# Second products of the gated feed-forward stages as seven block products, and their finish in another place: one Trainium2 core

## The chip, the cores and the metric

The kernel is one program on one core of a Trainium2 chip. Its time is the device time of one execution in microseconds (us). TensorE does the matrix products, VectorE (DVE), ScalarE (ACT) and GpSimd (POOL) the elementwise work, and SyncE (SP) issues the transfers from the chip's memory. Each engine runs its own instructions in the order in which they were written, and waits for others by semaphores.

## The reference

`reference` computes twelve half-layers on 512 tokens of width 1024, all in float32. Four of them are the gated feed-forward layers that the change touches:

```python
def swiglu_ffn(x, g, w_in, w_out):
    h = rms_norm(x, g)
    gate, up = jnp.split(h @ w_in, 2, axis=-1)
    return (jax.nn.silu(gate) * up) @ w_out
...
x = x + 0.5 * swiglu_ffn(x, ffn1_norm[layer], ffn1_w_in[layer], ffn1_w_out[layer])
```

`w_in` is 1024 x 5632 and `w_out` 2816 x 1024. The other stages are two mixers, and a second block of two layers whose modulation vector is `silu(c) @ w_mod + b_mod`, a 1024-vector by a 1024 x 6144 matrix for each layer.

## The kernel before

**Numbers.** Every float32 product is made of three products of rounded halves: each operand is split into a high part (ACT copies it to the type fp32r) and a low part (DVE subtracts the high part), and TensorE computes high x high, high x low and low x high. Names end in `h` and `l` for the two parts.

**Units.** Weights come in *units* of 128 x 1024 (or 128 x 768) in one stream for the whole program, numbered u. SP loads unit u into `raw[u % 4]` (RING = 4) when the unit four before it has been split; ACT makes `wh[u % 4]` as soon as TensorE is through with unit u - 4 (step `load`, `weights(u)`), DVE makes `wl[u % 4]`. The steps are planned so that unit u + 3 (AHEAD = 3) is split while TensorE is at unit u. A unit of 128 x 1024 is 8 tiles, so 24 matmuls of 512 columns.

**A gated stage** (`F1_0`, `F2_0`, `F1_1`, `F2_1`) has 22 tiles of 128 of the inner width in three parts of 8, 8 and 6 (`PARTS`). For each tile there are a `gate` and an `up` unit (a *pair*). Step `evac` finishes a tile: DVE multiplies both products by `rstd` from PSUM, ACT applies silu, POOL multiplies, ACT makes `a0h` or `a1h` and DVE `a0l` or `a1l` (two buffers, by part). Step `down` multiplies one unit of `w_out` with the tiles of a part and `add` adds half of it to `x`. `plan_ffn` writes the order: gate and up of parts 0 and 1, down of part 0, gate and up of part 2, down of part 1, down of part 2. So 16 units stand between the last tile of a part and the use of it, or 8 for part 2.

**Modulation.** DVE computes the modulation vectors on the side in the gated stages: 54 steps `mod` each, of which 48 are a *fold* (one weight tile of 256 KB, loaded by SP into one of three slots when the fold three before it is done) and 6 a transpose and a sum. A pair has one, a down unit two.

**Groups.** The ungated stages (`REL_0`, `REL_1`) already have their second products in *groups*: two output tiles, two times 4 tiles of the inner width, and two halves of the tokens (`SOONER`, `LATER`) make a product of 2 x 2 blocks by 2 x 2 blocks, done with seven block products instead of eight, as Strassen's method does. It needs sums of weight blocks (`first_sum` to `fourth_sum`, then their high and low parts in `low_sums`, `low_fourth`, `low_dif`) and sums of blocks of `a` (`t`, kept in `a1h` and `a1l`), and afterwards sums of the results. There the weight sums of a group are made in two sets of slots while TensorE is in the group before it.

## Time and profile before

| | |
|---|---|
| runs | 3074.09 us median of 3 (3073.77 to 3079.27) |
| the profiled execution | 3072.16 us, of which 3070.4 us are the span from the first to the last instruction |
| granted clock of TensorE | 0.997 of full speed |
| TensorE busy | 3035.4 us, 99% |
| VectorE busy | 1884.7 us, 61% |
| ScalarE busy | 1168.8 us, 38% |
| DMA | 33.2% of 16 engines, 107 GB/s |

Matmuls overlap in the profile: one lasts 390 ns, but the next starts before it ends, so what one costs is the distance from start to start. The same holds in a smaller measure on VectorE and ScalarE, where instructions in a row start some 0.09 us before the one ahead has ended. Rows of the line of time have the start first and then how long.

### The profile page before, as it was taken

The page shows a single profiled execution, that of the slowest core. Times are in us where ns is not written, and L with a number is a line of the kernel's source. Part 1 is how long each engine was busy: PE and PEld are TensorE (multiplying, and loading weights), DVE is VectorE, ACT ScalarE, POOL GpSimd, SP SyncE. Part 2 cuts the span into 40 slices and gives each one's busy share as a digit, 9 for nine tenths or more (in the row PEclk, how much of TensorE's full clock was granted, in tenths as well). Part 3 has the DMA queues.
Part 4 walks back from the last instruction along what each step waited for, and adds up shares of the span by engine and source line. Part 5 has one row for each costly group of instructions (what it writes and reads, how often), then busy time and mean ns, then how long its engine had stood idle before and what let it go on. Part 6 is the DMA issues. An engine that isn't in the chain of part 4 may idle for free.

```text
span 3070.4 us, 39047 instructions
## 1 busy us (share of the span) xinstructions
PE 3035.4 (99%) x15394; PEld 2499.0 (81%) x15394; DVE 1884.7 (61%) x2899; ACT 1168.8 (38%) x1877; POOL 670.0 (22%) x525
## 2 busy tenths in 40 slices
PE   9999999999999999999999999999999999999999
PEld 7888887788888888887778888776799977779997
DVE  6454557554555445536774455677777856877775
ACT  4322334333223322234443222446544334654442
POOL 2101134111011110044311100346211123721111
PEclk9999999999999999999999999999999999999999
DMA  5343432243443434431133344310333232033232
GB/s 191 117 154 123 127 98 73 86 140 118 155 130 115 137 117 154 134 108 62 35 127 117 120 155 134 115 37 21 107 103 110 98 110 67 20 95 110 97 102 77
DMA packets 115814, 329.86 MB, mean 107 GB/s; under 512 B 13616, under 2 KB 19120, under 8 KB 115248
## 3 DMA queue, kind: packets, MB, share of 16 engines
q1 hardware_dynamic: 115632, 327.36, 33.2%
q8 instruction: 123, 2.02, 0.3%
q14 instruction: 59, 0.48, 0.1%
HBM read 325.21 MB, written 2.10 MB: 107 GB/s over the span
## 4 chain that ended last, share of the span: by engine, by line
PE 92%; DVE 4%; ACT 2%; POOL 1%; issue 1%; DMA 0%; SPq 0%; DVEq 0%; ACTq 0%; POOLq 0%
PE ps L83 91%; PE ps L86 1%; ACT s_tmp L89 1%; POOL s_tmp L100 1%; DVE s_wl L92 1%; DVE s_tmp L92 1%; DVE s_tmp L112 0%; DVE s_x L95 0%; ACT s_wh L89 0%; DVE s_small L106 0%; DVE s_tmp L100 0%; POOL s_tmp L92 0%; DVE s_tmpr L92 0%; ACT s_hh L89 0%; DMA s_raw<-in_f1i_dram 0%
## 5 line engine op out<-in xcount | busy, mean ns | idle before, releaser
L83 PE MATMUL ps<-s_hh,s_wh 128*128 128x512 f32 x2304 | 894.6, 393 | 20.2 <-ACT s_hh L89 11.6
L89 ACT ACTIVATE s_wh<-s_raw 128x1024 fp32r<-128x1024 f32 (+3 forms) x560 | 530.6, 951 | 951.9 <-PE ps L83 949.7
L83 PE MATMUL ps<-s_hh,s_wl 128*128 128x512 f32 x2304 | 888.2, 391 | 0.2
L83 PE MATMUL ps<-s_hl,s_wh 128*128 128x512 f32 x2304 | 887.3, 390 | 0.0
L92 DVE TENSOR_TENSOR s_wl<-s_raw,s_wh 128x1024 fp32r<-128x1024 f32 (+3 forms) x529 | 595.9, 1127 | 428.1 <-ACT s_wh L89 427.5
L92 POOL TENSOR_TENSOR s_tmp<-s_tmp 128x512 f32<-128x512 f32 (+2 forms) x228 | 306.8, 1350 | 1692.6 <-ACT s_tmp L89 1531.7
L83 PEld LDWEIGHTS ps<-s_hh,s_wh 128*128 128x128 f32 x2304 | 433.3, 188 | 117.6 <-issue 16.8
L83 PEld LDWEIGHTS ps<-s_hh,s_wl 128*128 128x128 f32 x2304 | 433.9, 188 | 93.2 <-DVE s_wl L92 2.5
L83 PEld LDWEIGHTS ps<-s_hl,s_wh 128*128 128x128 f32 x2304 | 434.1, 188 | 90.9 <-issue 2.2
L83 PE MATMUL ps<-s_a0h,s_wh 128*128 128x512 f32 (+1 forms) x1024 | 381.8, 373 | 0.0
L83 PE MATMUL ps<-s_a0h,s_wl 128*128 128x512 f32 (+1 forms) x1024 | 378.4, 370 | 0.0
L83 PE MATMUL ps<-s_a0l,s_wh 128*128 128x512 f32 (+1 forms) x1024 | 378.4, 370 | 0.0
L83 PEld LDWEIGHTS ps<-s_a0h,s_wh 128*128 128x128 f32 x1024 | 193.0, 188 | 33.9 <-issue 1.3
L83 PEld LDWEIGHTS ps<-s_a0h,s_wl 128*128 128x128 f32 x1024 | 193.0, 188 | 32.8
L83 PEld LDWEIGHTS ps<-s_a0l,s_wh 128*128 128x128 f32 x1024 | 193.1, 189 | 32.6 <-DVE s_a0l L92 0.7
L92 DVE TENSOR_TENSOR s_a0l<-s_tmp,s_a0h 128x512 fp32r<-128x512 f32 (+1 forms) x120 | 79.8, 665 | 162.5 <-ACT s_a0h L89 162.5
L95 DVE SCALAR_TENSOR_TENSOR s_x<-ps,s_x 128x512 f32<-128x512 f32 x129 | 88.2, 684 | 118.9 <-PE ps L83 118.9
L83 PE MATMUL ps<-s_a1h,s_wh 128*128 128x512 f32 (+1 forms) x448 | 153.9, 344 | 0.0
L83 PE MATMUL ps<-s_a1l,s_wh 128*128 128x512 f32 (+1 forms) x448 | 153.9, 344 | 0.0
L83 PE MATMUL ps<-s_a1h,s_wl 128*128 128x512 f32 (+1 forms) x448 | 153.9, 344 | 0.0
L89 ACT ACTIVATE s_tmp<-ps 128x512 f32<-128x512 f32 (+6 forms) x258 | 132.3, 548 | 51.8 <-DVE s_tmp L92 20.1
L89 ACT ACTIVATE s_a0h<-s_tmp 128x512 fp32r<-128x512 f32 (+1 forms) x120 | 70.8, 590 | 190.2 <-POOL s_tmp L92 177.2
(167 smaller groups left out, 3618.7 us busy)
## 6 DMA issues: line engine op xcount, KB each, us to landing
s_raw<-in_ff_dram SPq DMA_DIRECT2D x128, 512.0 KB, 3.7
s_tmp<-in_w_mod_dram SPq DMA_DIRECT2D x192, 256.0 KB, 3.6
s_raw<-in_f1i_dram SPq DMA_DIRECT2D x88, 512.0 KB, 3.6
s_raw<-in_f2i_dram SPq DMA_DIRECT2D x88, 512.0 KB, 3.6
s_raw<-in_f1o_dram SPq DMA_DIRECT2D x32, 512.0 KB, 3.5
s_raw<-in_f2o_dram SPq DMA_DIRECT2D x32, 512.0 KB, 3.6
s_raw<-in_hyb_dram SPq DMA_DIRECT2D x28, 512.0 KB, 3.5
s_raw<-in_nsa_dram SPq DMA_DIRECT2D x28, 512.0 KB, 3.6
```

The lines of the kernel that those rows point to most:

```text
L83: return self.eng.matmul(o, w, m, **kw) if self.eng is not None else Blank()
L86: return self.eng.transpose(*a) if self.eng is not None else Blank()
L89: return self.eng.activation(o, a, f, **kw) if self.eng is not None else Blank()
L92: return self.eng.tensor_tensor(o, a, b, f) if self.eng is not None else Blank()
L95: return self.eng.scalar_tensor_tensor(o, a, s, b, f, g) if self.eng is not None else Blank()
L100: return self.eng.tensor_scalar(o, a, s, t, f) if g is None else self.eng.tensor_scalar(o, a, s, t, f, g)
```

## The change

In the gated stages the second product of parts 0 and 1 is made in groups (`lone_group`), four for each part; part 2 stays as it was. A group is two units of `w_out` and has seven blocks of 12 matmuls of 256 columns, 84 in all, where two down units had 48 of 512. `a0h` and `a0l` now hold every part, and `a1h` and `a1l` the block sums, so a part's products must be over before the next part's tiles are stored: the order becomes gate and up of part 0 and of the first tile of part 1, groups of part 0, the rest of part 1 and the first tile of part 2, groups of part 1, the rest of part 2, down of part 2.

There is one set of slots for weight sums (slots 45, 46, 48, 49, `ssum` and `ssum2`), and a group's own sums are made in the group. `raw` of a group's two units is given back to SP by the semaphore step of `low_fourth` (`raw_free`). The blocks that need `low_sums` and `low_fourth` stand last in TensorE's order. The finish of a tile is split: `evac` keeps the two DVE multiplications, silu and the product on POOL, and `fine`, after the next unit, makes the high and low parts and, for each second tile of parts 0 and 1, the block sums. The folds have two slots instead of three; no fold stands in a group, three in a pair of part 0, two in one of part 1, and four in each of four pairs of part 2. `lone_sum` adds up the kept blocks: for two output pairs right after the groups of part 1, for the two others in pairs of part 2.

```diff
+    def gate_up(p, these):
+        for i in these:
+            n = (sum(PARTS[:p]) + tile_of(p, i)) * 2
+            order.append((("gate", p, i), [stream.add(win[n], 1024)]))
+            order.append((("up", p, i), [stream.add(win[n + 1], 1024)]))
+    def down(p):
+        k0 = sum(PARTS[:p])
+        for d in range(0, KT, 2):
+            us = [stream.add(wout[d + m, :, k0 * 128:(k0 + PARTS[p]) * 128], PARTS[p] * 128) for m in range(2)]
+            if p == 2:
+                order.extend((("down", p, d + m), [us[m]]) for m in range(2))
             else:
-                steps.extend([("gate", p, t, ug), ("load", ug + AHEAD)])
-            if p == 0 and t == int(late_norm):
+                stream.group(us, True)
+                order.append((("group", p, d), us))
+    gate_up(0, range(8))
+    for p in (0, 1):
+        gate_up(p + 1, range(1))
+        down(p)
+        gate_up(p + 1, range(1, PARTS[p + 1]))
+    down(2)
...
+    for what, us in order:
+        kind, p, i = what
+        n = us[0] + AHEAD
+        steps.append((kind, p, i, us[0]))
+        if kind == "group":
+            if p == 1 and i == KT - 2:
+                steps.extend([("sum", 4), ("sum", 6)])
+            continue
+        if added:
+            steps.append(("add",) + added)
+        if n not in stream.second:
+            steps.append(("load", n))
+        if kind == "gate":
...
+            steps.append(("evac",) + before)
+        elif kind == "up":
+            fold(1 if i == 0 else (3, 2, 4)[p])
+            steps.append(("fine",) + before)
+            before = (p, i)
+            if p == 2 and i in (1, 2):
+                steps.append(("sum", 2 * i - 2))
+        elif before:
+            steps.extend([("evac",) + before, ("fine",) + before])
+            before = None
+        if n in stream.second:
+            steps.append(("load", n))
+        if added:
+            steps.append(("tile", added[1]))
+        if kind == "down":
...
+            added = (p, i)
+    steps += [("add",) + added, ("tile", added[1])]
...
         def raw_free(u):
-            if u in stream.first:
-                return g_lo[u + 1, 2]
-            return g_lo[u, 2] if u in stream.second else lo_of(u)
+            v = u + 1 if u in stream.first else u
+            return lo_of(u) if v not in stream.second else g_lo[v, 1 if v in stream.lone else 2]
         parity = {u: n % 2 for n, u in enumerate(sorted(stream.second))}
...
+            def lone_group(s, p, d, u0):
+                u1 = u0 + 1
+                c0, c1 = u0 % RING, u1 % RING
+                b0, b1, b2, b3 = group_at[u0]
+                claim(b0)
+                block(b0, LATER, wh[:, c0, 0:T], wl[:, c0, 0:T], w_hi[u0], w_lo[u0], a_part(s, p, 0, LATER))
+                block(b0, SOONER, wh[:, c1, 0:T], wl[:, c1, 0:T], g_hi[u1, 2], g_lo[u1, 2], t_part(s, p, 2)).then_inc(
+                    *g_mm.up((u0, 0)))
+                free[b0] = [(x_add, (s, p, d, "71"))]
+                claim(b1)
+                block(b1, LATER, wh[:, c0, T:2 * T], wl[:, c0, T:2 * T], w_hi[u0], w_lo[u0], a_part(s, p, 4, LATER)).then_inc(
+                    *unit.up(u0))
+                claim(b2)
+                block(b2, LATER, wh[:, c1, T:2 * T], wl[:, c1, T:2 * T], w_hi[u1], w_lo[u1], t_part(s, p, 3)).then_inc(
+                    *unit.up(u1))
+                free[b2] = [(x_add, (s, p, d + 1))]
+                claim(b3)
+                block(b3, SOONER, sums_hi(u1)[:, 0, :], sums_lo(u1)[1][:, 0, :], g_hi[u1, 0], g_lo[u1, 0], t_part(s, p, 0))
+                block(b3, LATER, sums_hi(u1)[:, 1, :], sums_lo(u1)[1][:, 1, :], g_hi[u1, 0], g_lo[u1, 0], t_part(s, p, 1)).then_inc(
+                    *g_mm.up((u0, 1)))
+                free[b3] = [(x_add, (s, p, d, "56"))]
+                block(b1, SOONER, fourth_hi(u1), fourth_lo(u1)[1], g_hi[u1, 1], g_lo[u1, 1], a_part(s, p, 4, SOONER)).then_inc(
+                    *g_mm.up((u0, 2)))
+                free[b1] = [(x_add, (s, p, d))]
             def group(s, p, d, u0):
...
+                    elif kind == "group":
+                        u0 = step[3]
+                        sums(u0 + 1)
+                        weights(u0 + 3)
+                        weights(u0 + 4)
+                    elif kind == "fine":
+                        _, p, i = step
+                        t, o = tile_of(p, i), S(33 + 2 * ((i + sum(PARTS[:p])) % 3))
+                        cols = LATER if p < 2 and t < 4 else slice(0, T)
+                        act.wait_ge(*prod[s, p, i])
+                        if p and i == 0:
+                            act.wait_ge(*unit[group_end[s, p - 1]])
+                            act.wait_ge(*g_mm[group_end[s, p - 1] - 1, 2])
+                        if p == 2 and i == 0:
+                            act.wait_ge(*x_add[s, "sum", 7])
+                        act.activation(a0h[:, t, cols], o[:, cols], ACT.Copy).then_inc(*a_hi.up((s, p, t)))
+                        if i % 2 and p < 2:
+                            for m in range(2):
+                                act.wait_ge(*t_dif[s, p, i // 2, (2, 3)[m]])
+                                act.activation(a1h[:, i // 2 * 2 + m, :], tmp[:, 24 + i // 2 * 2 + m, :], ACT.Copy).then_inc(
+                                    *t_hi.up((s, p, i // 2, m)))
                     elif kind == "tile":
                         tile(s + 1, step[1])
...
+            def lone_group(s, p, d, u0):
+                u1, n = u0 + 1, u0 + 3
+                b0, b1, b2, b3 = group_at[u0]
+                r0, r1 = PAIRS_FFN[d]
+                def keep(to, b, key):
+                    if p == 0:
+                        i = dve.tensor_scalar(to, two(B(b)), 1.0, None, ALU.mult)
+                    else:
+                        i = dve.tensor_tensor(to, two(B(b)), to, ALU.add)
+                    i.then_inc(*x_add.up(key))
+                first_sum(u1)
+                second_sum(u1)
+                fourth_sum(u1)
+                low_sums(u1)
+                dve.wait_ge(*g_mm[u0, 0])
+                keep(r0, b0, (s, p, d, "71"))
+                low_fourth(u1)
+                weights(n)
+                dve.wait_ge(*unit[u1])
+                dve.scalar_tensor_tensor(x[:, d + 1, LATER], ps[:, b2, LATER], 0.5, x[:, d + 1, LATER], ALU.mult,
+                                         ALU.add).then_inc(*x_add.up((s, p, d + 1)))
+                weights(u0 + 4)
+                dve.wait_ge(*g_mm[u0, 1])
+                keep(r1, b3, (s, p, d, "56"))
+                dve.wait_ge(*g_mm[u0, 2])
+                dve.scalar_tensor_tensor(x[:, d, :], B(b1), 0.5, x[:, d, :], ALU.mult, ALU.add).then_inc(*x_add.up((s, p, d)))
+            def lone_sum(s, d):
+                r0, r1 = PAIRS_FFN[d]
+                dve.wait_ge(*x_add[s, 1, d])
+                dve.tensor_tensor(r1[:, 1, :], r1[:, 1, :], r0[:, 1, :], ALU.add).then_inc(*x_add.up((s, d, "16")))
+                dve.scalar_tensor_tensor(x[:, d, LATER], r0[:, 1, :], 0.5, x[:, d, LATER], ALU.mult, ALU.add).then_inc(
+                    *x_add.up((s, d, "1")))
+                dve.wait_ge(*x_add[s, d, "16"])
+                dve.tensor_tensor(r1[:, 0, :], r1[:, 0, :], r1[:, 1, :], ALU.add).then_inc(*x_add.up((s, d, "165")))
+                dve.wait_ge(*x_add[s, d, "165"])
+                dve.scalar_tensor_tensor(x[:, d, SOONER], r1[:, 0, :], 0.5, x[:, d, SOONER], ALU.mult, ALU.add).then_inc(
+                    *x_add.up((s, "sum", d)))
+                dve.wait_ge(*x_add[s, "sum", d])
...
@@ -2075,12 +2243,26 @@
                             u = unit_at[s, ("gate", "up")[m], p, t]
                             dve.wait_ge(*unit[u])
                             dve.tensor_tensor(S(o), B(bank_of[u]), rstd[:, :], ALU.mult).then_inc(*gate_up_.up((s, p, t, m)))
...
+                    elif kind == "fine":
+                        _, p, i = step
+                        n, t = i + sum(PARTS[:p]), tile_of(p, i)
+                        o = S(33 + 2 * (n % 3))
+                        cols = LATER if p < 2 and t < 4 else slice(0, T)
+                        if i % 2 and p < 2:
+                            dve.wait_ge(*prod[s, p, i])
+                            block_sums(s, p, i // 2, S(33 + 2 * ((n - 1) % 3)), o)
                         dve.wait_ge(*a_hi[s, p, t])
-                        dve.tensor_tensor(ahl[p % 2][1][:, t, :], S(j), f32(ahl[p % 2][0][:, t, :]),
-                                          ALU.subtract).then_inc(*a_lo.up((s, p, t)))
+                        dve.tensor_tensor(a0l[:, t, cols], o[:, cols], f32(a0h[:, t, cols]), ALU.subtract).then_inc(*a_lo.up((s, p, t)))
+                        if i % 2 and p < 2:
+                            low_block_sums(s, p, i // 2)
                     elif kind == "add":
                         _, p, d = step
...
             def mod_load(f, n):
                 l, c, k = f // 2, 6 * (f % 2) + n // KT, n % KT
-                if n >= 3:
-                    sp.wait_ge(*mod_acc[(f,) + divmod(n - 3, KT)])
-                sp.dma_start(S(43 + n % 3), ins["w_mod"][l, k * 128:(k + 1) * 128, c * T:(c + 1) * T]).then_inc(
-                    *mod_in[n % 3].up((f, n), 16))
+                if n >= 2:
+                    sp.wait_ge(*mod_acc[(f,) + divmod(n - 2, KT)])
+                sp.dma_start(S(43 + n % 2), ins["w_mod"][l, k * 128:(k + 1) * 128, c * T:(c + 1) * T]).then_inc(
+                    *mod_in[n % 2].up((f, n), 16))
             def table(name, dst, src, key):
                 sp.dma_start(dst, src).then_inc(*tab_in[name].up(key, 16))
...
+                at_, split = steps[s][0][1], set()
                 for step in steps[s]:
                     kind = step[0]
-                    if kind == "load":
-                        weights(step[1] + RING)
-                    elif kind == "mod" and step[2] < KT and 8 * step[1] + step[2] + 3 < 48:
-                        mod_load(f, 8 * step[1] + step[2] + 3)
+                    if kind == "load" and step[1] not in stream.first | stream.second:
+                        split.add(step[1])
+                    elif kind == "group":
+                        split |= {step[3], step[3] + 1} | ({step[3] + 3, step[3] + 4} - stream.first - stream.second)
+                    elif kind == "mod" and step[2] < KT and 8 * step[1] + step[2] + 2 < 48:
+                        mod_load(f, 8 * step[1] + step[2] + 2)
+                    while at_ in split:
+                        weights(at_ + RING)
+                        at_ += 1
             def hyb(s):
```

VectorE at the last down units of part 0, before: for each unit an addition to `x`, the low part of a unit of weights and two folds.

```order
L95 SCALAR_TENSOR_TENSOR s_x<-ps,s_x 128x512 [waits pe_unit]
L92 TENSOR_TENSOR s_wl<-s_raw,s_wh 128x1024 [waits act_w_hi]
L95 SCALAR_TENSOR_TENSOR s_tmp<-s_tmp,s_c_act 128x512 [waits dve_mod_acc,in_mod2]
L95 SCALAR_TENSOR_TENSOR s_tmp<-s_tmp,s_c_act 128x512 [waits dve_mod_acc,in_mod0]
L95 SCALAR_TENSOR_TENSOR s_x<-ps,s_x 128x512 [waits pe_unit]
```

VectorE in the second group of part 0 after the change, from `first_sum` to the addition to `x` (`act_w_hi` is raised by ScalarE's copy of a unit, which waits for that unit's transfer):

```order
L96 TENSOR_TENSOR s_tmp<-s_raw 128x512
L96 TENSOR_TENSOR s_tmp<-s_tmp,s_raw 128x512 [waits dve_g_sum]
L96 TENSOR_TENSOR s_ssum<-s_raw,s_tmp 128x512 [waits dve_difference]
L96 TENSOR_TENSOR s_tmpr<-s_tmp,s_tmpr 128x1024 [waits act_sum_hi,dve_difference]
L104 TENSOR_SCALAR s_tmp<-ps 128x512 [waits pe_group]
L96 TENSOR_TENSOR s_ssum_r<-s_ssum,s_ssum_r 128x512 [waits act_sum_hi]
L96 TENSOR_TENSOR s_wl<-s_raw,s_wh 128x512 [waits act_w_hi]
L96 TENSOR_TENSOR s_wlf<-s_raw 128x512 [waits in_raw3,in_raw2]
L96 TENSOR_TENSOR s_wl<-s_wlf,s_wh 128x512 [waits act_sum_hi]
L99 SCALAR_TENSOR_TENSOR s_x<-ps,s_x 128x256 [waits pe_unit]
L96 TENSOR_TENSOR s_wl<-s_raw,s_wh 128x1024 [waits act_w_hi]
```

The folds are gone from here, and the `s_wl` of 128x1024, the first unit of the group after next, now stands behind a wait for ScalarE at the end of a row of eleven instructions; the keeping of the second pair of blocks and an addition to `x` follow it.

SyncE's queue at the end of part 0 after the change, where the transfers of the groups begin:

```order
L128 DMA s_tmp<-in_w_mod_dram 128x512 [waits dve_mod_acc] x4
L128 DMA s_raw<-in_f1o_dram 128x1024 [waits dve_sum_lo]
L128 DMA s_raw<-in_f1o_dram 128x1024
L128 DMA s_raw<-in_f1o_dram 128x1024 [waits dve_sum_lo]
L128 DMA s_raw<-in_f1o_dram 128x1024
L128 DMA s_raw<-in_f1i_dram 128x1024 [waits dve_sum_lo]
```

The units of `w_out` went out one by one before, each behind a `dve_w_lo`; now they go out in twos behind `dve_sum_lo`, the semaphore of `low_fourth`.

VectorE at the end of the gate and up pairs of a stage after the change, up to the first down unit of part 2; the last tile's finish was ahead of the eight down units of part 1 before:

```order
L99 SCALAR_TENSOR_TENSOR s_tmp<-s_tmp,s_c_act 128x512 x3
L90 STREAM_TRANSPOSE s_tmp<-s_tmp 128x512
L110 TENSOR_REDUCE s_nsm<-s_tmp 128x16
L96 TENSOR_TENSOR s_a0l<-s_tmp,s_a0h 128x512
L96 TENSOR_TENSOR s_wl<-s_raw,s_wh 128x768
L96 TENSOR_TENSOR s_tmp<-ps,s_rstd 128x512 x2
L96 TENSOR_TENSOR s_wl<-s_raw,s_wh 128x768
L96 TENSOR_TENSOR s_a0l<-s_tmp,s_a0h 128x512
L96 TENSOR_TENSOR s_wl<-s_raw,s_wh 128x768
L96 TENSOR_TENSOR s_tmp<-ps,s_rstd 128x512 x2
L96 TENSOR_TENSOR s_a0l<-s_tmp,s_a0h 128x512
L99 SCALAR_TENSOR_TENSOR s_x<-ps,s_x 128x512
```

The multiplications and the low part of the last two tiles now stand directly ahead of the first addition of part 2, with a unit of weights between them.

## Rows read from the trace of the kernel before

**Rows 1.** The page: busy time and its share of the span.

```profile
PE 3035.4 (99%) x15394; PEld 2499.0 (81%) x15394; DVE 1884.7 (61%) x2899; ACT 1168.8 (38%) x1877; POOL 670.0 (22%) x525
```

**Rows 2.** The chain of waits in order of time: start, how long, what.

```profile
9.97 411.07 PE ps L83 x1815
```

**Rows 3.** Line of time of TensorE in `REL_0`: starts of a group and of the next.

```profile
2227.14 0.28 PE L83 MATMUL ps<-s_a0h,s_wh 128*128 128x256 f32 x1
...
2237.22 0.28 PE L83 MATMUL ps<-s_a0h,s_wh 128*128 128x256 f32 x1
```

**Rows 4.** Line of time of VectorE in `REL_0`, ahead of and in the first groups.

```profile
2219.02 1.56 DVE L92 TENSOR_TENSOR s_tmp<-s_tmp 128x256 f32<-128x256 f32 x4 [0.93 <-POOL s_tmp L92]
...
2222.30 0.69 DVE L92 TENSOR_TENSOR s_tmp<-s_raw 128x512 f32<-128x512 f32 x1
2223.09 0.69 DVE L92 TENSOR_TENSOR s_tmp<-s_tmp,s_raw 128x512 f32<-128x512 f32 x1
2223.82 0.69 DVE L92 TENSOR_TENSOR s_tmp<-s_raw,s_tmp 128x512 f32<-128x512 f32 x1
2224.99 1.83 DVE L92 TENSOR_TENSOR s_tmpr<-s_tmp,s_tmpr 128x1024 fp32r<-128x1024 f32 x2 [0.47 <-ACT s_tmpr L89]
...
2227.34 0.68 DVE L92 TENSOR_TENSOR s_wlf<-s_raw 128x512 f32<-128x512 f32 x1
2228.72 0.69 DVE L92 TENSOR_TENSOR s_wl<-s_wlf,s_wh 128x512 fp32r<-128x512 f32 x1 [0.70 <-ACT s_wh L89]
...
2237.48 0.75 DVE L95 SCALAR_TENSOR_TENSOR s_x<-ps,s_mod,s_x 128x512 f32<-128x512 f32 x1
2238.14 1.22 DVE L92 TENSOR_TENSOR s_wl<-s_raw,s_wh 128x1024 fp32r<-128x1024 f32 x1
2239.28 0.48 DVE L95 SCALAR_TENSOR_TENSOR s_x<-ps,s_mod,s_x 128x256 f32<-128x256 f32 x1
```

**Rows 5.** Issues of transfers, KB each, us to landing: of 2229.44 us, and the page's.

```profile
s_raw<-in_ff_dram SPq DMA_DIRECT2D x1, 512.0 KB, 3.7
...
s_tmp<-in_w_mod_dram SPq DMA_DIRECT2D x192, 256.0 KB, 3.6
```

**Rows 6.** Line of time of VectorE in `F1_0`, a pair of part 1.

```profile
273.13 1.23 DVE L92 TENSOR_TENSOR s_wl<-s_raw,s_wh 128x1024 fp32r<-128x1024 f32 x1 [2.80 <-ACT s_wh L89]
274.27 1.28 DVE L92 TENSOR_TENSOR s_tmp<-ps,s_rstd 128x512 f32<-128x512 f32 x2
277.68 0.69 DVE L92 TENSOR_TENSOR s_a0l<-s_tmp,s_a0h 128x512 fp32r<-128x512 f32 x1 [2.13 <-ACT s_a0h L89]
```

**Rows 7.** The same pair on ScalarE: silu, high part, next weights.

```profile
274.99 0.63 ACT L89 ACTIVATE s_tmp<-s_tmp 128x512 f32<-128x512 f32 x1 [1.89 <-DVE s_tmp L92]
277.02 0.63 ACT L89 ACTIVATE s_a0h<-s_tmp 128x512 fp32r<-128x512 f32 x1 [1.40 <-POOL s_tmp L92]
277.56 1.04 ACT L89 ACTIVATE s_wh<-s_raw 128x1024 fp32r<-128x1024 f32 x1
```

**Rows 8.** VectorE in `F1_0` at down units: folds, a transpose and its sum.

```profile
300.40 1.60 DVE L95 SCALAR_TENSOR_TENSOR s_tmp<-s_tmp,s_c_act 128x512 f32<-128x512 f32 x2
...
312.35 0.70 DVE L86 STREAM_TRANSPOSE s_tmp<-s_tmp 128x512 f32<-128x512 f32 x1
...
313.69 0.48 DVE L100 TENSOR_SCALAR s_tmp<-s_tmp,s_c_act 128x512 f32<-128x512 f32 x1
```

**Rows 9.** VectorE in `REL_0`: one sum-up of kept blocks, and what follows it.

```profile
2435.91 0.88 DVE L92 TENSOR_TENSOR s_mix_tmp<-s_mix_tmp 128x256 f32<-128x256 f32 x2
...
2439.07 1.22 DVE L92 TENSOR_TENSOR s_wl<-s_raw,s_wh 128x1024 fp32r<-128x1024 f32 x1
```

**Rows 10.** Three stretches: length, busy by engine (x instructions), TensorE's granted clock, DMA.

```profile
1947.90:1951.70 3.80, 0.15 (x1) 0.01 (x1) 2.08 (x6) 3.70 (x10) 0.00 (x0) 0.83 0.57 148
1951.70:1957.00 5.30, 5.28 (x13) 4.13 (x14) 4.72 (x6) 1.53 (x2) 3.74 (x5) 0.50 0.94 355
2163.60:2172.00 8.40, 5.50 (x21) 3.80 (x22) 7.27 (x12) 4.78 (x8) 0.00 (x0) 1.00 0.62 189
```

More of the change, by code:

```diff
@@ L176, in down @@
-    def down(p, before):
-        k0 = sum(PARTS[:p])
-        for d in range(KT):
-            u = stream.add(wout[d, :, k0 * 128:(k0 + PARTS[p]) * 128], PARTS[p] * 128)
-            steps.append(("down", p, d, u))
-            if d:
-                steps.append(("add", p, d - 1))
-            steps.append(("load", u + AHEAD))
-            if before:
-                steps.append(("evac",) + before)
-                before = None
-            if p == 2 and d:
-                steps.append(("tile", d - 1))
-            if p < 2:
-                fold(2)
-            elif d == 2:
-                steps.append(("modsum",))
-        steps.append(("add", p, KT - 1))
-        if p == 2:
-            steps.append(("tile", KT - 1))
@@ new lines, in plan_ffn @@
+    gate_up(0, range(8))
[4 more added lines that the diff above has]
+    down(2)
+    ug, uu = (order.pop(0)[1][0] for _ in range(2))
+    steps += [("load", ug + AHEAD), ("first", ug, uu), ("load", uu + AHEAD)]
+    if not late_norm:
+        steps.append(("norm",))
+    fold(1)
+    before, added = (0, 0), None
+    for what, us in order:
[11 more added lines that the diff above has]
+        if kind == "gate":
+            if late_norm and (p, i) == (0, 1):
+                steps.append(("norm",))
+            steps.append(("evac",) + before)
[13 more added lines that the diff above has]
+        if kind == "down":
+            if i == 2:
+                steps.append(("modsum",))
+            added = (p, i)
```

176 lines of the change are left out of this document (95 added, 81 removed).

## The prediction

> **What bounds the kernel now.** The page first: TensorE is busy 99% of the span, VectorE 61%, ScalarE 38% [rows 1]. The chain of waits says the same: it is long runs of matmuls with no other engine between them, 1815 in 411.07 us, so 0.2265 us for one of 512 columns [rows 2]. So a cut in TensorE's work counts in full, but there is no slack: any wait of TensorE is a loss. I then read the line of time of `REL_0`, the stage that has groups already, for what a group asks of each engine, and that of `F1_0` for the pairs, and last what the clock does after idle time.
>
> **What TensorE saves.** A group of 84 matmuls of 256 columns starts 10.08 us after the one ahead of it [rows 3], 0.120 us each. Two down units are 48 x 0.2265 = 10.88. So a group saves 0.80, a stage with eight groups 6.4, the four stages 25.6. Nothing else changes on TensorE.
>
> A rule of the Trainium skill ("TensorE: Matmul & The Clock Gate", Back-to-back issue gap) gives columns/2.4 GHz plus 2.5 ns, so 215.8 and 109.2 ns; a group would then save 1.19 us. The rows have 226.5 and 120, and the sum keeps them.
>
> **VectorE in a group.** In `REL_0` the sums are made one group ahead; here they are made in the group. From starts in [rows 4], with t = 0 at `first_sum`: second 0.79, fourth 1.52, `low_sums` 2.69 (ends 3.91: two halves of 1.83 less the overlap), `keep` of block pair 71 at 3.82, `low_fourth` 4.42, done at 5.11. That semaphore gives both raw buffers back, and SP issues. The unit lands 3.65 later [rows 5], t = 8.79. ScalarE splits it in 1.06 [rows 7], and VectorE's low part of unit u0+4 starts at 9.9 and takes 1.14 to the next start [rows 4, 6]. Behind it in VectorE's order stand the keeping of pair 56 (0.6) and an addition (0.6): the next `first_sum` comes at t = 12.26. Without the transfer wait the same row of work would end near 10.36. TensorE needs 10.08. So each group comes 12.26 - 10.08 = **2.18** later than the one ahead, and TensorE waits for it in block 56, which needs `low_sums`: 6.0 us after the group's start (4 blocks of 12 and a fetch), with 4.1 us of matmuls after it. A transfer is thus freed and wanted within one group.
>
> The skill ("DMA: Bandwidth & Descriptors", Anatomy of one DMA, SWDGE path) has about 2.0 us of fixed cost plus bytes over 436 GB/s: 3.2 us for 512 KB instead of the row's 3.7. The cycle would be 11.8, and the groups still late.
>
> **Part 0.** A pair has three folds with two slots. The third fold's load starts when the first is done and takes 3.6 [rows 5]; with 0.75 for a fold [rows 8] it starts 4.38 after the first, and the three take 5.0. Add the low parts of two units, the two multiplications (starts 1.14 and 1.28 on, [rows 6]) and the tile's finish; the odd tile's, with its block sums (six operations of 128 x 256 or their like, [rows 4]), I put at 3.28. VectorE comes to the first group with `first_sum` at P + 2.95, P being the end of the pairs on TensorE. There it wants `low_sums` by P + 6.0: 2.95 + 3.91 = 6.9, so 0.9 late, then three times 2.18: **7.4**.
>
> **Part 1.** Two folds, both loaded in time: `first_sum` at P + 0.75, from three multiplications that stand behind the last matmul. The first group is on time, the others together 0.84 + 2 x 2.18 = **5.2**.
>
> **The end of a stage.** This is where most goes. When TensorE ends the last group of part 1, VectorE has 4.24 us left in it (t = 12.26 against P at t = 8.02). Then stand two `lone_sum` of 3.2 each [rows 9] and five pairs, TensorE's part of which is 48 x 0.2265 = 10.9 us each. In four of them VectorE has four side steps with two slots: four folds take 5.9, since the third and the fourth wait for loads of 3.6; three with a transpose and its sum (1.34, [rows 8]) 4.8 to 6.6, by where it stands. That is 23.2 for the four; two low parts of weights, two multiplications and a finish are 2.3 + 2.5 + 0.7 in each, 22; two more `lone_sum` 6.4. So 4.2 + 6.4 + 23.2 + 22 + 6.4 = 62.2, and 3.5 of waits for ScalarE and POOL as in [rows 6, 7]: tile (2,4) has its high part at P + 65.7. The last tile (2,5), in a pair without folds, has it at P + 70.8, and its low part at P + 71.5. Down unit 0 of part 2 needs both and would end at P + 54.4 + 4.1 = P + 58.5 unstalled. Before, eight down units, 87 us, lay between the last tile and its use; now there is one unit of weights. So TensorE stands **13.5** us: 71.5 - 58.5, and half a microsecond of matmuls that follow the last operand. Some 1.5 of it falls earlier, at the weights of the last pairs. Even with VectorE on time, the last tile costs: multiplication, silu 0.63, POOL, high part 0.63 [rows 7]: 3.4 from the first multiplication to the high part's end, 4.1 to the low part's; 277.68 - 274.27 in [rows 6] is that chain. It is exposed for 2.3.
>
> **The clock.** The stall falls in pieces of about 6.7 and 4.2 us. After 3.8 us of near idleness TensorE ran 5.3 us at a granted 0.50, 1.2 GHz; after 2.8 idle us it kept 1.00 [rows 10]. One such stretch for each stage costs half of some 5 us: **2.5**. The stalls inside groups are near 2 us each and leave it.
>
> **Sum.** For a stage 7.4 + 5.2 + 13.5 + 2.5 - 6.4 = 22.2; for four 88.8. The profiled execution took 3072.16, 2 us under the median, so 3161; I say **3160**. What a measurement here can tell from no change is about 0.2%, 6 us.
>
> Costed at nothing: POOL's work (22% busy, [rows 1]), and ScalarE's extra copies of block sums, which stand beside VectorE's folds. If ScalarE's order in a group (high sums, then `weights(u0+3)`) held VectorE back by 0.3, 20 groups would add 6. The issues of SP now wait for `low_fourth` in twos, and a w_mod load stands behind them in its queue; I count it as landed by the pair's first fold, and if it isn't, the end of a stage is another 2 later.
>
> **Rivals.**
> - *Loads of folds land in time.* Their 3.6 us [rows 5] may be spent behind the transposes, finishes and `lone_sum`s, if VectorE is so late that SP is far ahead. Then a pair of part 2 has 3.0 of folds instead of 5.9, and the end costs 5.2 instead of 13.5, the groups as above: 7.4 + 5.2 + 5.2 + 2.5 - 6.4 = 13.9, times four 56: **3128**. Against it: two slots and four folds in a row leave nothing else to do between the first and the third. Chance 0.17.
> - *The groups are not held by transfers* (cycle 10.36, 0.28 late each), only the end is late: 0.9 + 3 x 0.28 = 1.7 in part 0, 0 in part 1, at the end 13.5 - 1.9 = 11.6, since VectorE leaves the groups that much sooner, and 2.5 for the clock. Less 6.4 that is 9.4 a stage, 38 in all: **3110**. For it: in [rows 4] the unit that is split behind a group's additions starts with no wait. Against: there it was loaded a group earlier. Chance 0.1.
> - *Faster: VectorE's lateness does not reach TensorE* but at the last tile: 1.7 + 2.3 - 6.4 = -2.4 a stage, near **3062**, and 3072.2 - 25.6 = 3046.5 with no stall at all. It decides when VectorE's cycle in a group is under about 10.3 and the four folds of a pair under 4.5. For it: VectorE has 39% idle [rows 1], and a stage 360 us to spread it. Against: its order is fixed, and the waits computed above are for transfers, not for room. Chance 0.1.
> - *The short matmuls bring nothing*, when operands change with each one: at 0.1295 instead of 0.120 the 6.4 is gone. The pitch is from 84 in a row with the same change of operands [rows 3], so little speaks for it. **3186**. Chance 0.05.
> - No change within 0.2%: only where the waits chance to be 6.4 a stage, 0.02.
>
> **How the numbers follow.** The likeliest case has 0.56, with a range of its own of 3140 to 3180, from 1.9 to 2.4 for a group's lateness (20 of them, 5 either way) and 11 to 16 for an end (10 either way). The range of 8 in 10 takes in the 3128 and the 3110, with room below for an end that is shorter than its sum, and ends at the top short of the case without gain: 3096 to 3182. Faster, the fourth case, 0.1; same 0.02; slower 0.88, all the others.
>
> **What would show it.** In the profile after: matmuls of 256 columns about 0.120 apart, 2688 more of them and 1536 fewer of 512; TensorE waiting in every group but the first of part 1 for VectorE's write of `tmpr`, 2.2 us; VectorE idle about 1.5 in a group on ScalarE's `wh`, and about 3 us in each pair of part 2 on transfers of w_mod; TensorE idle over 10 us before or in the first down unit of part 2 for `a0h` or `a0l`, and PEclk dips there in four places. VectorE's busy share should grow by few points only. If VectorE shows no idle on `wh` in groups, the group cycle is wrong; if the folds of part 2 follow one another with no gap, the end is.

## The result and the profile after

| | before | changed |
|---|---|---|
| runs | 3075.51 us median of 4 (3073.77 to 3079.27) | 3159.33 us median of 4 (3156.39 to 3167.49) |
| changed / before | | 1.0275, 95% interval 1.0253 to 1.0297 |
| the profiled execution's span | 3070.4 us | 3165.4 us |
| granted clock | 0.997 | 0.985 |

The changed kernel is 2.75% slower, 84 us; 3160 was forecast. The first line of its page answers to [rows 1]:

```profile
PE 3053.2 (96%) x16546; PEld 2551.1 (81%) x16546; DVE 2192.8 (69%) x3491; ACT 1246.6 (39%) x2037; POOL 671.5 (21%) x525
```

TensorE has fewer columns to work through and is busy longer, and the granted clock is lower, so part of its work ran at the low clock; and 112 us of the span are without its work, where 35 were. Whom it waits for (the view of waits of TensorE: total, times, longest):

```profile
PE ps L87 <- ACT s_a0h L93: 25.2, 8, 3.4
PE ps L87 <- DVE s_tmpr L96: 16.5, 23, 0.8
PE ps L87 <- ACT s_tmpr L93: 12.9, 17, 1.5
PE ps L87 <- ACT s_hh L93: 11.4, 4, 3.5
PE ps L87 <- DVE s_a0l L96: 11.4, 5, 3.2
```

`s_a0h` and `s_a0l` are the last tiles of part 2, three waits in each gated stage; `s_tmpr` are a group's own weight sums. Further down stand 5.2 us on `s_a1h` and 2.8 on `s_a1l`, the block sums of a part's last tiles, all in the first groups of part 0. (`s_hh` is the start of the ungated stages.) Now one gated stage, `F2_0`, by windows. A window goes from the first matmul of a part's second product to the first behind it. Columns: length, busy (x instructions) of TensorE, its weight loads, VectorE, ScalarE, GpSimd, then the granted clock, DMA share, GB/s. Before the change, the eight units of part 0, and the units of parts 1 and 2 together:

```profile
794.47:837.99 43.52, 43.52 (x193) 36.04 (x192) 28.16 (x36) 9.64 (x10) 1.29 (x1) 1.00 0.54 175
903.27:979.87 76.60, 76.60 (x346) 63.15 (x344) 46.55 (x61) 24.46 (x32) 11.97 (x8) 1.00 0.44 133
```

After it: groups of part 0, groups of part 1, the pairs of part 2, down units of part 2:

```profile
743.96:792.33 48.37, 43.73 (x337) 42.16 (x336) 37.17 (x56) 15.05 (x20) 0.00 (x0) 0.96 0.25 85
879.39:924.58 45.19, 41.56 (x337) 40.59 (x336) 34.12 (x49) 13.90 (x18) 0.00 (x0) 1.00 0.26 86
924.58:980.24 55.66, 55.01 (x242) 44.91 (x241) 41.47 (x65) 14.36 (x18) 5.18 (x4) 1.00 0.46 145
980.24:1027.08 46.84, 37.76 (x154) 28.94 (x152) 26.82 (x36) 18.60 (x27) 13.22 (x9) 0.85 0.33 107
```

Four groups take 48.37 and 45.19 us where eight units took 43.52; without a wait they take 40.27, as an experiment below shows. The down units of part 2 took 76.60 - 43.52 = 33.08 and take 46.84, 9.1 of it idle and 4.7 in matmuls that are longer at a mean clock of 0.85. The four gated stages together grew from 1390.7 to 1478.3 us, 87.6 in the two profiled executions. (The profiled one of the changed kernel was the longest of its four; the rest of its surplus lies outside the gated stages.)

The place where a group loses its time, VectorE in the third group of part 0 of `F2_0`, from `first_sum` to the next group's:

```profile
772.57 0.68 DVE L96 TENSOR_TENSOR s_tmp<-s_raw 128x512 f32<-128x512 f32 x1
...
775.17 1.23 DVE L96 TENSOR_TENSOR s_tmpr<-s_tmp,s_tmpr 128x1024 fp32r<-128x1024 f32 x1 [0.47 <-ACT s_tmpr L93]
...
779.50 0.69 DVE L96 TENSOR_TENSOR s_wl<-s_wlf,s_wh 128x512 fp32r<-128x512 f32 x1 [0.70 <-ACT s_wh L93]
780.11 0.42 DVE L99 SCALAR_TENSOR_TENSOR s_x<-ps,s_x 128x256 f32<-128x256 f32 x1
781.96 1.23 DVE L96 TENSOR_TENSOR s_wl<-s_raw,s_wh 128x1024 fp32r<-128x1024 f32 x1 [1.44 <-ACT s_wh L93]
783.10 0.68 DVE L104 TENSOR_SCALAR s_mix_tmp<-ps 128x512 f32<-128x512 f32 x1
783.70 0.68 DVE L99 SCALAR_TENSOR_TENSOR s_x<-ps,s_x 128x512 f32<-128x512 f32 x1
784.30 0.68 DVE L96 TENSOR_TENSOR s_tmp<-s_raw 128x512 f32<-128x512 f32 x1
```

and ScalarE, whose copy VectorE waits for at 781.96:

```profile
780.86 1.06 ACT L93 ACTIVATE s_wh<-s_raw 128x1024 fp32r<-128x1024 f32 x1 [1.40 <-DMA s_raw<-in_f2i_dram]
```

VectorE stands on ScalarE, ScalarE stands on the transfer, and behind it in VectorE's row are a `keep`, an addition and only then the next `first_sum`. From `first_sum` to `first_sum` it is 11.73 us here and 12.1 on the mean of all 24 such distances in the gated stages (11.6 to 12.9); TensorE has work for 10.07.

The end of the same stage on TensorE, only the matmuls that waited:

```profile
985.34 0.50 PE L87 MATMUL ps<-s_a0l,s_wh 128*128 128x512 f32 x1 [2.67 <-DVE s_a0l L96]
...
989.47 0.80 PE L87 MATMUL ps<-s_a0h,s_wh 128*128 128x512 f32 x1 [3.40 <-ACT s_a0h L93]
...
994.46 0.80 PE L87 MATMUL ps<-s_a0h,s_wh 128*128 128x512 f32 x1 [3.02 <-ACT s_a0h L93]
```

Three tiles in a row come late: VectorE is behind with their finish. And its folds ahead of it:

```profile
971.46 0.75 DVE L99 SCALAR_TENSOR_TENSOR s_tmp<-s_tmp,s_c_act 128x512 f32<-128x512 f32 x1 [2.49 <-DMA s_tmp<-in_w_mod_dram]
972.57 0.75 DVE L99 SCALAR_TENSOR_TENSOR s_tmp<-s_tmp,s_c_act 128x512 f32<-128x512 f32 x1 [0.36 <-DMA s_tmp<-in_w_mod_dram]
...
982.46 0.75 DVE L99 SCALAR_TENSOR_TENSOR s_tmp<-s_tmp,s_c_act 128x512 f32<-128x512 f32 x1 [2.42 <-DMA s_tmp<-in_w_mod_dram]
```

### The profile page after: what moved, and what is told of

The parts are those of the page before. It is cut to its first block, busy times and chain, and to the rows that moved or that the text cites. A ratio compares the mean times of both kernels' runs of the same rounds, so it can differ in the third digit from the quotient of the medians.

```text
span 3165.4 us, 42171 instructions
## 1 busy us (share of the span) xinstructions
PE 3053.2 (96%) x16546; PEld 2551.1 (81%) x16546; DVE 2192.8 (69%) x3491; ACT 1246.6 (39%) x2037; POOL 671.5 (21%) x525
## 4 chain that ended last, share of the span: by engine, by line
PE 66%; DVE 16%; DMA 6%; ACT 5%; issue 5%; POOL 2%; DVEq 0%; SPq 0%; ACTq 0%; POOLq 0%
PE ps L87 65%; DVE s_tmp L96 4%; DVE s_wl L96 3%; DMA s_tmp<-in_w_mod_dram 3%; ACT s_wh L93 3%; DVE s_tmp L99 2%; PE ps L90 1%; DVE s_x L99 1%; ACT s_tmpr L93 1%; POOL s_tmp L104 1%; DVE s_tmpr L96 1%; ACT s_tmp L93 1%; DMA s_raw<-in_f1o_dram 1%; DMA s_raw<-in_f2o_dram 1%; DMA s_raw<-in_f1i_dram 1%
## 5 line engine op out<-in xcount | busy, mean ns | idle before, releaser
L93 ACT ACTIVATE s_wh<-s_raw 128x1024 fp32r<-128x1024 f32 (+3 forms) x560 | 516.0, 924 | 524.7 <-PE ps L87 440.4
L87 PE MATMUL ps<-s_a0h,s_wh 128*128 128x512 f32 (+1 forms) x1024 | 361.5, 353 | 25.2 <-ACT s_a0h L93 25.2
L87 PE MATMUL ps<-s_a0l,s_wh 128*128 128x512 f32 (+1 forms) x1024 | 358.3, 350 | 11.2 <-DVE s_a0l L96 11.2
L87 PE MATMUL ps<-s_a0h,s_wl 128*128 128x512 f32 (+1 forms) x1024 | 356.4, 348 | 0.0
L93 ACT ACTIVATE s_tmp<-s_tmp 128x512 f32<-128x512 f32 (+1 forms) x98 | 61.2, 627 | 381.4 <-DVE s_tmp L96 381.3
L87 PE MATMUL ps<-s_a1h,s_tmpr 128*128 128x256 f32 x896 | 179.7, 292 | 29.6 <-DVE s_tmpr L96 16.2
L99 DVE SCALAR_TENSOR_TENSOR s_tmp<-s_tmp,s_c_act 128x512 f32<-128x512 f32 x168 | 125.6, 747 | 94.7 <-DMA s_tmp<-in_w_mod_dram 88.0
L87 PEld LDWEIGHTS ps<-s_a1h,s_tmpr 128*128 128x128 f32 x896 | 146.8, 196 | 37.9 <-DVE s_tmpr L96 21.9
L93 ACT ACTIVATE s_tmpr<-s_tmp 128x1024 fp32r<-128x1024 f32 (+1 forms) x120 | 96.4, 826 | 202.6 <-DVE s_tmp L96 178.4
L96 DVE TENSOR_TENSOR s_tmp<-s_tmp 128x256 f32<-128x256 f32 (+4 forms) x344 | 151.7, 476 | 24.4 <-POOL s_tmp L96 20.2
```

What stands on the lines that cost most here:

```text
L87: return self.eng.matmul(o, w, m, **kw) if self.eng is not None else Blank()
L93: return self.eng.activation(o, a, f, **kw) if self.eng is not None else Blank()
L96: return self.eng.tensor_tensor(o, a, b, f) if self.eng is not None else Blank()
L99: return self.eng.scalar_tensor_tensor(o, a, s, b, f, g) if self.eng is not None else Blank()
```

## The experiments

The theory: two transfers that are freed and wanted within one stretch of VectorE's row (a group's raw buffers; the two fold slots) make VectorE late, and TensorE with it. The rivals: VectorE simply has too much work there, or the new order alone does the harm. All kernels but where it is said are the changed kernel with one edit. The lengths in this table are windows of `F2_0` as above, in us.

| kernel | median | to before (95%) | groups p. 0 | groups p. 1 | pairs of p. 2 | down p. 2 |
|---|---|---|---|---|---|---|
| before | 3075.5 | | 43.52 | 43.52 | 54.4 | 33.08 |
| changed | 3159.3 | 1.0275 (1.0253 to 1.0297) | 48.37 | 45.19 | 55.66 | 46.84 |
| e1_free | 3101.5 | 1.0086 (1.0071 to 1.0101) | 42.37 | 40.27 | 54.41 | 43.04 |
| e10_late | 3125.2 | 1.0164 (1.0147 to 1.0181) | 44.22 | 41.84 | 54.41 | 45.86 |
| e2_folds | 3131.5 | 1.0180 (1.0165 to 1.0195) | 48.02 | 48.18 | 54.41 | 35.74 |
| e6_ungroup | 3091.5 | 1.0050 (1.0035 to 1.0065) | 43.52 | 43.52 | 54.40 | 37.32 |
| e4_free_folds | 3088.5 | 1.0042 (1.0027 to 1.0057) | 42.53 | 42.77 | 54.41 | 35.73 |
| e5_all3 | 3086.1 | 1.0037 (1.0023 to 1.0051) | 42.33 | 42.43 | 54.42 | 35.73 |
| e7_split | 3070.7 | 0.9988 (0.9979 to 0.9997) | 41.80 | 42.75 | 54.42 | 33.07 |
| e8_best | 3050.3 | 0.9923 (0.9909 to 0.9937) | 40.26 | 40.27 | 54.41 | 33.07 |

**e1_free: the raw buffers given back by their last reader.** `low_fourth`, whose semaphore frees them, reads `ssum` and not `raw`; the last reader is `fourth_sum`.

```diff
         def raw_free(u):
             v = u + 1 if u in stream.first else u
-            return lo_of(u) if v not in stream.second else g_lo[v, 1 if v in stream.lone else 2]
+            if v in stream.lone:
+                return g_dif[v, 1]
+            return lo_of(u) if v not in stream.second else g_lo[v, 2]
```

> One change to the changed kernel: the two raw buffers of a group's units are given back to SP by the semaphore of fourth_sum, the last instruction that reads them, and not by that of low_fourth, 2.9 us later in VectorE's row. Theory (a transfer that is freed and wanted within one group makes the group's cycle): unit u0+4 lands before ScalarE and VectorE come to it, the cycle falls from 12.1 to about 10.2, only the first group of part 0 is late, and VectorE leaves part 1 some 2 to 4 us sooner; 13 to 15 us less a stage, 3100 to 3107. Rival (the order of VectorE's row and ScalarE's copies make the cycle, the transfer only fills it): no group gets shorter, over 3150.

3101.5, within the theory's span: 58 us for one semaphore. VectorE in the same place of a group:

```profile
738.46 0.69 DVE L96 TENSOR_TENSOR s_wlf<-s_raw 128x512 f32<-128x512 f32 x1
739.85 0.69 DVE L96 TENSOR_TENSOR s_wl<-s_wlf,s_wh 128x512 fp32r<-128x512 f32 x1 [0.70 <-ACT s_wh L93]
740.45 0.42 DVE L99 SCALAR_TENSOR_TENSOR s_x<-ps,s_x 128x256 f32<-128x256 f32 x1
740.79 1.23 DVE L96 TENSOR_TENSOR s_wl<-s_raw,s_wh 128x1024 fp32r<-128x1024 f32 x1
```

The low part of unit u0+4 follows with no wait, and `first_sum` comes every 10.22 or 10.23 us in all 24 cases. The groups of part 1 take 40.27, TensorE's own time. The rival is out. The end of the stage is still 10 us too long (43.04).

**e10_late: the wait left, its followers taken from behind it.**

```diff
-                weights(u0 + 4)
                 dve.wait_ge(*g_mm[u0, 1])
                 keep(r1, b3, (s, p, d, "56"))
                 dve.wait_ge(*g_mm[u0, 2])
                 dve.scalar_tensor_tensor(x[:, d, :], B(b1), 0.5, x[:, d, :], ALU.mult, ALU.add).then_inc(*x_add.up((s, p, d)))
+                weights(u0 + 4)
```

> One change to the changed kernel, on VectorE alone: in a group the low part of unit u0+4, which waits for that unit's transfer, stands behind the keeping of pair 56 and the addition to x and not ahead of them. The transfer is issued and lands as before. Theory (the wait for the transfer, with 1.2 us of other work queued behind it, makes the group's cycle): the two instructions go into the wait, the cycle falls from 12.1 to 10.9, each late group is 1.2 us less late, and VectorE leaves part 1 1.2 us sooner: 5 to 7 us a stage less, 3130 to 3140. Rival (VectorE's work, not a wait, fills the cycle): no change, 3155 to 3163.

3125.2, 34 us less than the changed kernel and 5 better than the theory's span. The distance of `first_sum`s fell to 11.0 on the mean (10.5 to 11.8, but for one of 12.2). No work was taken away, so the cycle was a wait. The estimate had added up its own terms too low: three distances of 1.2 us less in each of two parts, and 1.2 at the end, are 8.4 a stage and not 5 to 7. Measured, on the mean of the four stages, are 3.8 in part 0, 3.2 in part 1, 0.6 in the pairs of part 2 and 1.2 at the end. In part 0 of `F2_0` a stretch at the low clock is gone too (1.00 where it was 0.96); in part 0 of `F1_0` it is longer (6.8 us instead of 3.4), so the clock is not shown to be the surplus.

```profile
736.20:780.42 44.22, 41.81 (x338) 40.60 (x337) 37.47 (x56) 15.05 (x20) 0.00 (x0) 1.00 0.27 93
```

**e2_folds: fewer folds where their loads can't keep up.**

```diff
-            fold(1 if i == 0 else (3, 2, 4)[p])
+            fold(1 if i == 0 else (3, 3, 2)[p])
```

> One change to the changed kernel: folds stand three in a pair of part 0, three in one of part 1 and two in one of part 2 (3, 2 and 4 before), so 9 side steps instead of 16 lie between the groups of part 1 and the last tile. Theory (third and fourth folds wait for loads into two slots): some 14 us of VectorE's time in part 2 go, so the stall of 11 us ahead of the last operands and most of its slow-clock stretch go too; about 2 us of exposed last finish stay, and part 1's first group gets up to 2 us later: 3115 to 3127. Rival (VectorE is late there by the amount of its work): 7 folds of 0.75 are 5.3 us a stage, 3135 to 3140.

3131.5 lies between the two spans, 4 us from the theory's. The windows say why: the end of `F2_0` did what the theory said (46.84 to 35.74, clock 1.00), but part 1, with the third fold moved into its pairs, went from 45.19 to 48.18, 3.0 us where I had put up to 2 (3.0 to 4.6 in the four stages). Seven folds of 0.75 are 5.3 us; the end and the pairs of `F2_0` gave back 12.4. Not all of that is time in which VectorE waited for loads: some 2.9 of it are the slow matmuls behind the last wait, which went with the wait.

```profile
872.73:920.91 48.18, 42.49 (x338) 40.75 (x336) 37.01 (x56) 15.04 (x20) 0.00 (x0) 1.00 0.23 81
975.32:1011.06 35.74, 33.66 (x154) 27.04 (x152) 21.91 (x27) 16.73 (x24) 11.12 (x8) 1.00 0.32 102
```

**e6_ungroup: the new order without groups.** Parts 0 and 1 have down units as before the change; no weight sums, no block sums, no `lone_sum`. The edit's core (tiles are finished with all their columns again, and additions to `x` follow each unit):

```diff
-            if p == 2:
+            if True:
                 order.extend((("down", p, d + m), [us[m]]) for m in range(2))
...
-        elif before:
+        elif before and p == 2:
             steps.extend([("evac",) + before, ("fine",) + before])
```

> The changed kernel's order, finish in two steps, two fold slots and places of folds, but the second products of parts 0 and 1 made unit by unit as before the change (no groups, no weight sums, no block sums, no lone_sum). Theory (groups and sums make VectorE late; the order alone exposes the last finish): TensorE loses the 6.4 us a stage again, waits nowhere in parts 0 and 1, and at the end of a stage 2 to 5 us: 3084 to 3098. Rival 1 (the order itself, with four folds in a pair, makes the 14 us at the end): over 3120. Rival 2 (the order costs nothing): 3075.

3091.5, in the theory's span. The end is 4.2 us long here (37.32 - 33.08; 4.2 to 4.6 in the four stages, 17.4 in all), not 14. TensorE waits for the last tile's finish alone, 1.85 us for its high part (2.19 in `F1_0`) and 0.22 for its low part, as it does in e2_folds with half the folds; the rest is a stretch of 3.4 us at a granted 0.50 that follows this wait in all four stages:

```profile
953.78:991.10 37.32, 35.24 (x154) 28.20 (x152) 20.88 (x27) 16.72 (x24) 11.69 (x8) 0.95 0.34 103
```

VectorE waits 93.7 us for the loads of folds in this kernel, more than the 88.0 in the changed one, and TensorE is not held by it. So these waits do harm only on top of the lateness from the groups and of four `lone_sum`s; which of the two is the larger share no run separates. The price of the order alone is 2.7 us for the exposed finish and 1.6 for the clock behind it, in the run some 16 us.

**e5_all3 and e4_free_folds: the repairs together.** e4 is e1's and e2's edit; e5 has besides `third_sum` ahead of `low_sums`, in VectorE's wait for ScalarE:

```diff
                 fourth_sum(u1)
+                if n in stream.second:
+                    third_sum(n)
                 low_sums(u1)
...
-                weights(n)
+                weights(n, True)
```

> Three changes to the changed kernel: raw freed by fourth_sum; third_sum moved ahead of low_sums in a group, where it fills VectorE's wait for ScalarE (0.47 us) and takes away the later one (0.70); folds 3, 3, 2. Theory: the group's cycle is 9.1 us, under TensorE's 10.08, so no group but the first of each part waits, and the end costs about 3 us: the saving of 6.4 a stage shows but for 4 to 6 us: 3065 to 3080. Rival (something else than these waits holds the groups, such as the transfers' own rate with the units of 512 KB in twos): over 3095.

> Two of the three changes: raw freed by fourth_sum and folds 3, 3, 2, with third_sum where the changed kernel has it. Theory: with the raw buffers freed early the cycle of a group is 10.2 us, so third_sum's new place (9.1) is worth only what lateness the first group of a part hands on: 0 to 2 us a part, so 3086 to 3098 against the 3086 of all three. Rival (third_sum's new place carries the gain): over 3100.

e4 gave 3088.5, as the theory had it: `third_sum`'s place is worth 2 us, less than the two can be told apart by. But e5 missed its span by 6 us. It loses 9.3 us a stage where 4 to 6 were expected. The end, put at about 3, is 35.73 - 33.08 = 2.7 in `F2_0` and `F1_1`, but 4.4 and 4.3 in `F1_0` and `F2_1`, where a stretch at the low clock follows the wait for the last tile. And the first groups of the two parts cost 5.8 and not 1 to 3: the worst is `F1_0`, whose groups of part 0 take 47.75 us and not 42.33, since the first one waits 3.2 us for the block sums of the last tiles, and the clock falls behind it.

```profile
109.30:115.80 6.50, 3.05 (x22) 2.56 (x20) 5.51 (x11) 3.25 (x5) 0.00 (x0) 0.98 0.14 39
115.80:122.00 6.20, 5.69 (x25) 5.39 (x26) 6.13 (x10) 2.62 (x4) 0.00 (x0) 0.50 0.34 104
```

**e7_split: the last tile multiplied last** (e5, and):

```diff
-                        product(b, u, natural(s, p), range(PARTS[p]), True, True).then_inc(*unit.up(u))
+                        last = PARTS[p] - 1
+                        if d < 2:
+                            product(b, u, natural(s, p), range(last), True, False)
+                            if d:
+                                product(bank_of[u - 1], u - 1, natural(s, p), [last], False, True).then_inc(*unit.up(u - 1))
+                                product(b, u, natural(s, p), [last], False, True).then_inc(*unit.up(u))
+                        else:
+                            product(b, u, natural(s, p), range(PARTS[p]), True, True).then_inc(*unit.up(u))
```

> The kernel with the three changes (raw freed by fourth_sum, third_sum moved, folds 3, 3, 2), and in it the last tile of part 2 multiplied last: down units 0 and 1 of part 2 go over tiles 0 to 4 each, then both over tile 5, so 6.8 us of matmuls and not 3.4 stand ahead of the last tile's use. Theory (what is left at the end of a stage is the exposed finish of the last tile): the 2.0 to 2.4 us of waiting for its high part go in all four stages, 8 to 10 us, 3076 to 3079. Rival (VectorE and ScalarE are still late there for other work, such as the weights of the down units): 0 to 3 us less, over 3083.

The end is 33.07 in all four stages, TensorE's own time: what was left there was the last tile's finish, and the low clock behind the wait for it. The time fell to 3070.7, 15.4 below e5 where 8 to 10 were expected. The estimate had counted the wait alone: the four ends of e5 are 14.0 us over TensorE's own time, not four times 2.0 to 2.4. The groups are 2.8 shorter besides, 1.8 of that in part 0 of `F1_0` (45.99).

**e8_best: the finish ahead of the first groups** (e7, and):

```diff
+        early = kind == "up" and p and i == 0
+        if early:
+            steps.append(("fine",) + before)
         if n not in stream.second:
             steps.append(("load", n))
...
-            fold(1 if i == 0 else (3, 3, 2)[p])
-            steps.append(("fine",) + before)
+            fold(0 if i == 0 else 2 + int(i < (7, 7, 4)[p]))
+            if not early:
+                steps.append(("fine",) + before)
```

> The same with two more moves: in the pair that stands between a part's last tile and its groups, that tile's finish with its block sums comes ahead of the next unit's weights and no fold stands there; folds are 3 in a pair and 2 in the last pair of parts 0 and 1, in part 2 three, three, three, two, two. Theory (what is left in the groups is the first group of each part, waiting 1 to 4 us for the block sums of the last tiles): these waits go but for 1 us, and TensorE's saving of 6.4 us a stage shows nearly whole: 3055 to 3064, faster than both kernels. Rival (the first group then waits for its own weight sums instead): 3068 to 3076.

3050.3, better than either span, and faster than the kernel before by 0.77% (0.63 to 0.91). The same windows of `F2_0`: TensorE busy all the time in each.

```profile
713.74:754.00 40.26, 40.26 (x337) 40.26 (x336) 34.67 (x49) 15.71 (x20) 0.00 (x0) 1.00 0.38 129
841.06:881.33 40.27, 40.27 (x338) 40.27 (x337) 34.79 (x50) 15.70 (x20) 0.00 (x0) 1.00 0.38 130
935.74:968.81 33.07, 33.07 (x153) 27.11 (x152) 21.21 (x29) 16.74 (x24) 11.73 (x8) 1.00 0.36 120
```

In the view of waits only 0.8 us on `s_tmpr` are left of the waits in groups, and none on `s_a0h`. The groups of the four stages were 20.6 us over TensorE's own time in e7 and are 0.8 here. The gain of 23.7 us is TensorE's 26.0 less 2.3; in the two profiled executions the gated stages are 25.1 us shorter. VectorE still waits for loads of folds, 113.8 us in 40 places, more than in the changed kernel, and none of it reaches TensorE. VectorE is busy 34.7 of 40.3 us in the groups, 86%: there was room for the sums in the group, though little.

## Why the prediction was right

Term by term, for a stage, on the mean of the four. Lateness is what a window has over 40.27 us for the groups and over 33.08 and 54.41 at the end; there, the stall is counted up to the last matmul that waits, and the clock is what the matmuls behind it lose:

| step | forecast | measured |
|---|---|---|
| TensorE's saving | -6.4 | -6.5 (e8_best: 2 x 40.27 against 2 x 43.52) |
| lateness in part 0 | 7.4 | 8.8 (7.6 to 10.5) |
| lateness in part 1 | 5.2 | 5.2 (4.6 to 6.0) |
| the end of a stage: stall | 13.5 | 11.6 (10.9 to 12.6) |
| the same: clock | 2.5 | 2.7 (2.4 to 2.9) |
| sum | 22.2 | 21.9 |

The mechanism was right in each row. That the sum is right to 0.3 is in part luck: part 0 was 1.4 too low and the stall at the end 1.9 too high. For part 0, VectorE's finish of the odd tile in `F2_0` and the first `first_sum` behind it (TensorE begins the groups at 743.96):

```profile
744.76 1.54 DVE L96 TENSOR_TENSOR s_tmp<-s_tmp 128x256 f32<-128x256 f32 x4
746.22 0.68 DVE L96 TENSOR_TENSOR s_a0l<-s_tmp,s_a0h 128x512 fp32r<-128x512 f32 x1
746.82 1.29 DVE L96 TENSOR_TENSOR s_a1l<-s_tmp,s_a1h 128x512 fp32r<-128x512 f32 x2
748.02 0.68 DVE L96 TENSOR_TENSOR s_tmp<-s_raw 128x512 f32<-128x512 f32 x1
```

- **The saving** was right to 0.1: a 256-column matmul costs 40.27 / 336 = 0.1199 us. The 109.2 ns that the prediction worked out from the formula of the Trainium skill ("TensorE: Matmul & The Clock Gate", Back-to-back issue gap), an estimate for 256 columns, do not show in this kernel, even in e8_best, where nothing waits; the row taken from `REL_0` did. The fourth rival (no gain from short matmuls) is out.
- **The group's cycle** was put at 12.26 and is 12.1 (24 distances). e1 and e10 show that it is the wait for the transfer, with the work queued behind it: without the wait 10.22 (10.36 forecast), with the followers moved away 11.0 (10.9 expected). The 1.4 to 2.6 us of idle time ahead of `s_wl` stood at the place that the prediction named. A transfer of 512 KB of `w_out` still takes 3.7 us, as in the row; the 3.2 us that the prediction set beside it from the Trainium skill ("DMA: Bandwidth & Descriptors", Anatomy of one DMA, SWDGE path) are an estimate for transfers that GpSimd issues, and these are SyncE's.
- **Part 0** was 1.4 too low, and all of it is in the first group. The odd tile's finish with its block sums takes 3.26 us in the rows above (748.02 - 744.76), where 3.28 was forecast. But the first `first_sum` comes at P + 4.1 here, and at P + 4.0, 5.4 and 6.2 in the other stages, not at P + 2.95; the prediction does not show how it comes to 2.95, so which term is short stays open. With that the first group is 2.8 late on the mean and not 0.9, and the three others add 5.9 (6.5 forecast). TensorE spends this time on something that the sum has no wait for: the first group also needs the block sums of the last tiles, ahead of its weight sums, and stands 3.3 us on `a1h` and `a1l` in `F1_0`, 2.5 in `F2_1` and 1.1 in the other two. e8 shows it: with the finish moved ahead and the fold beside it taken out, the wait is gone.
- **The end**: the last tile's high part is there at P + 69.8 in `F2_0`, 1.0 sooner than forecast (P + 70.8), and TensorE takes it up at once, at P + 68.7 to P + 70.4 in the four stages; the forecast waited for the low part besides, which is made while the first matmuls of the tile run. The exposed finish alone is 2.7 (2.3 forecast; e4 and e2). The prediction did not separate what the groups, the folds and the `lone_sum`s have in the rest; e6 shows that none of it is there without the groups and their sums.
- **The clock in groups** was expected to stay up. It did not: four stretches of 3.4 us at a granted 0.50 stand in the groups of the changed kernel (part 0 of `F1_0`, `F2_0` and `F2_1`, part 1 of `F1_1`). They cost nothing that shows there: the lateness of each part is, within 0.1 us, what VectorE's row alone gives by the prediction's rule.
- **The first rival** (fold loads in time) did not come: VectorE waited 88.0 us for `w_mod` transfers in 34 places, at 3.3 us a load (median) and not 3.6. **The second** (groups not held by transfers) is what e1 makes of the kernel: 3101.5 where 3110 was worked out for it. **The third**, the faster one, had its condition right ("when VectorE's cycle in a group is under about 10.3 and the four folds of a pair under 4.5"): e4 meets it and is still 0.4% slower, since the first groups and the finish were counted too low there: 1.7 and 2.3 a stage, where e4 loses 6.4 and 3.1. It takes e7's and e8's edits as well.

## What to carry to other kernels

- Ask of each buffer which instruction reads it last, and free it by that one. Here the semaphore of an instruction that no longer read it, 2.9 us further down the row, cost 58 us.
- Work that saves time on the busiest engine can be paid for on another whose busy share is far from full: what counts is its row between a transfer's release and its use, and what is queued behind the wait.
- Where a change takes cover away (eight units between the last tile and its use), restore some by order: multiply the tile that is finished last after all others.
